# A two-block transformer kernel on one core: the order of the output projections at the end of the first block, and where the second branch's weights are loaded

## The chip, the cores and the metric

The kernel runs on one core of one Trainium2 chip. The metric is the device time of one execution in microseconds. All data is fp32, so each wide matmul of the program stands in the trace as two records.

## The reference

512 tokens of width 1024 go through two blocks. The change lies in the end of the first block's mixing half and the start of its expert half:

```python
merged = gate_a * (y_a @ w_branch_a[l]) + gate_b * (y_b @ w_branch_b[l])
mix = merged @ w_out[l]
x = layer_norm(DN_ALPHA * x + g1 * mix, ln1_g[l], ln1_b[l])
h = layer_norm(x) * (1 + sc2) + sh2
# moe_ffn(h): top 4 of 32 experts for each token
logits = (xt @ w_router).astype(jnp.float32) + b_router
top_v, top_e = lax.top_k(logits, TOP_K)
```

`y_b` is the attention's output (512 wide), `w_branch_b` is 512 x 1024, `w_out` 1024 x 1024, `w_router` 1024 x 32. The assignments are sorted by expert; each expert's rows are then read in blocks of 64. The second block (recurrent and attention mixing, then a product-key expert layer that gathers 128 rows for each token) is not touched.

## The kernel before

Each engine has its own instruction list, written out by hand, and they meet through semaphores. The program is a row of stages (`first_mix`, `first_merge`, `experts`, `second_project`, `second_heads`, `route_peer`); `end_stage` (line 57) clears the stage's semaphores and puts a barrier over all engines between two of them. Transfers that are under way are not waited for by the barrier.

Weights come in units of 512 columns into `ring`, three slots of 2 MB that lie in the same memory as the later expert weights `wt`. In `first_mix` a list of 17 names (line 121) is worked off: unit n goes into slot n % 3, and SP waits until the outputs of unit n - 3 are done (`s_full`). Four outputs of 128 x 512 are made of each unit, 68 in all. The last loop of TensorE takes two of the last eight projections (`gb0`, `gb1`, the second gate) for each of four token tiles, waits for the vector engine's combined attention output of the tile (`s_yb`) and transposes it into `yT[:, 1]`. For each tile SP first reads the three attention groups back from DRAM (line 348); the third read waits for the first tile to be combined, the fourth for the second.

`first_merge` (lines 814 to 1058) then does, with everything loaded anew from its start:

- The branch product: eight groups of 128 rows, four matmuls each (line 892), from `w_branch_b`'s halves in slots 0 and 1. The vector engine multiplies each by the gate and adds it to `mT` (lines 1013, 1014).
- `mixed(t)`, the output projection of token tile t (line 902): two halves of 8 matmuls, into two PSUM banks of its own, from `w_out`'s halves in slots 2 and 0. The second half of `w_out` is issued when the first four branch groups are done.
- `tile(t)` on the vector engine (lines 990 to 999): scales and adds the residual, norm, second norm, and writes `h2`. Each of the two norms sends its variance to ScalarE for a square root (`root(2t)`, `root(2t + 1)`, line 949).
- `logits(t)`: eight transposes of `h2` (line 910), two copies of them on ScalarE (`keep(t)`, line 954), and the router product, 8 narrow matmuls of 32 columns (line 916). `choose(t)` on the vector engine (lines 1003 to 1009) takes the top four and makes a mask.
- `rank(t)`: matmuls with triangular and all-ones matrices that count the assignments before each token (line 927), and in the last tile the total of each expert (line 924). After the last mask the vector engine works out `pos`, the row of each assignment (line 1047).
- GpSimd scatters the rows of `h2` to DRAM, sixteen indirect transfers of 512 KB (line 882). The stage ends when these have landed. SP issues the first expert's twelve weight units of 1 MB (line 870) as soon as the last `mixed` is done, since they lie over `ring` and `mT`.

The orders before: TensorE does mixed 0, mixed 1, logits 0, mixed 2, logits 1, mixed 3, logits 2, rank 0, rank 1, logits 3, rank 2, rank 3. The vector engine does tile 0, tile 1, choose 0, tile 2, choose 1, tile 3, choose 2, choose 3. ScalarE does roots 0, 1, 2, 3, keep 0, roots 4, 5, keep 1, roots 6, 7, keep 2, keep 3.

`experts` begins by reading the first gathered rows and transposing them (line 1144).

Of the kernel before, what the change touches and what calls it, by code (L numbers as in the profile page):

```python
# [13 lines left out]
P = 128  # L14
T = 512
NT = T // P
D = 1024
KD = D // P
W = 512
# [28 lines left out]
TAKEN = []  # L48
# [15 lines left out]
def build(nc, A, K, out, dram):  # L64

    with ExitStack() as ctx:
        def sb(name, shape, dt=F32, c=ctx):
            return c.enter_context(nc.sbuf_tensor(name, shape, dt))

        ident = sb("ident", [P, P])  # L70
        tri = sb("tri", [P, 4, P])
        mod = sb("mod", [P, 6 * D])
        x = sb("x", [P, NT, D])
        ps = ctx.enter_context(nc.psum_tensor("ps", [P, 8, W], F32))
        blocks = sb("blocks", [P, NBLK + 1 + NE], I32)
        pos = sb("pos", [P, NT, TOPK], I32)
        w4 = sb("w4", [P, NT, TOPK])
        with ExitStack() as early:
            wt = sb("wt", [P, NUNIT, 2, D], c=early)
            s_w = [nc.alloc_semaphore(f"e_w{u}") for u in range(NUNIT)]  # L80
            with ExitStack() as first:
                flat = wt[:, :, :, :].rearrange("p u k n -> p (u k n)")
                qkv = flat[:, 0:12 * D].rearrange("p (b a t w) -> p b a t w", b=2, a=3, t=NT)
                ring = flat[:, 12 * D:].rearrange("p (n k w) -> p n k w", n=3, k=KD)
                gB = flat[:, 0:KD * T].rearrange("p (f t) -> p f t", f=KD)
                mT = flat[:, 6 * D:6 * D + KD * T].rearrange("p (f t) -> p f t", f=KD)
                yT = sb("yT", [P, 2, NT, T], c=first)
                hT = sb("hT", [P, KD, T], c=first)
                first_mix(nc, A, K, dram, ident, tri, mod, x, ps, yT, hT, qkv, ring, mT, gB)
                end_stage(nc)  # L90
                first_merge(nc, A, K, dram, ident, tri, mod, x, ps, yT, hT, ring, mT, gB, blocks, pos, w4, wt, s_w)
                end_stage(nc)
            experts(nc, A, K, dram, ident, ps, blocks, wt, s_w)
            end_stage(nc)
        mix = sb("mix", [P, NT, D])
        uv = sb("uv", [P, NRING, 2, D])
        with ExitStack() as second:
            flat = uv[:, :, :, :].rearrange("p n a d -> p (n a d)")
            TA, NA = T + TC, NT + NTC
            ends = [0]  # L100
            for n in (8 * TA, NA * MH * (MD + 1), (NA + NT) * MH * MD, NA * 784):
                ends.append(ends[-1] + n)
            parts = [flat[:, a:b] for a, b in zip(ends, ends[1:])]
            S = dict(ct=parts[0], va=parts[1].rearrange("p (t h c) -> p t h c", t=NA, h=MH), ko=parts[2],
                     zr=parts[3].rearrange("p (t c) -> p t c", t=NA), bg=sb("bg", [P, 16], c=second), flat=flat)
            kept = (NT + NTC) * MH * MD
            S["kt"] = S["ko"][:, 0:kept].rearrange("p (t h c) -> p t h c", t=NT + NTC, h=MH)
            S["om"] = S["ko"][:, kept:].rearrange("p (t c) -> p t c", t=NT)
            second_project(nc, A, K, dram, ident, mod, x, ps, S, mix, pos, w4)
            end_stage(nc)  # L110
            s_wout = [nc.alloc_semaphore(f"q_wout{u}") for u in range(2)]
            second_heads(nc, A, K, dram, ident, tri, mod, ps, S, mix, s_wout)
            end_stage(nc)
        route_peer(nc, A, K, dram, ident, tri, mod, x, ps, mix, out, uv, s_wout)


def first_mix(nc, A, K, dram, ident, tri, mod, x, ps, yT, hT, qkv, ring, mT, gB):

    NB = 3
    names = ["u", "v"] + [f"{a}{g}" for g in range(3) for a in "qkV"] + ["ga0", "wa0", "ga1", "wa1", "gb0", "gb1"]  # L120
# [21 lines left out]
    with ExitStack() as ctx:  # L142
# [6 lines left out]
        with ExitStack() as ctx2:  # L149
# [63 lines left out]
            s_landed = [sem(f"landed{i}") for i in range(NB)]  # L213
# [57 lines left out]
            with nc.Block() as block:  # L271
                @block.sync
                def _(sp):
# [63 lines left out]
                    sp.wait_ge(s_rows, 1)  # L337
                    sp.dma_start(dram["modr"], rows).then_inc(s_rout, 16)
                    sp.wait_ge(s_rout, 16)
                    for b in range(2):  # L340
                        sp.wait_ge(s_out[b], outs_before[b])
                    for t in range(NT):
                        if t >= 2:
                            sp.wait_ge(s_yb, t - 1)
                        else:
                            sp.wait_ge(s_PT, 12)
                            sp.wait_ge(s_o, 12)
                        sp.dma_start(oc[:, t % 2], dram["o"][:, t * P:(t + 1) * P, :].rearrange("g p c -> p g c")
                                     ).then_inc(s_oc[t % 2], 16)

                @block.gpsimd
                def _(pool):
# [458 lines left out]
                        dve.tensor_tensor(y, y, oc[:, t % 2, 2, 0:AH * DH], ALU.add).then_inc(s_yb, 1)  # L811


def first_merge(nc, A, K, dram, ident, tri, mod, x, ps, yT, hT, ring, mT, gB, blocks, pos, w4, wt, s_w):

    NB = 3
    PAD = 16
    with ExitStack() as ctx:
        def sb(name, shape, dt=F32):
# [2 lines left out]
        def sem(name):  # L822
            return take(nc, "g_" + name)
# [24 lines left out]
        sw = small[:, 28:32]  # L848
        posf = small[:, 32:48].rearrange("p (t k) -> p t k", t=NT)

        s_landed = [sem(f"landed{i}") for i in range(NB)]
        s_const, s_back, s_full, s_gate, s_branch, s_mix = (sem(n) for n in ("const", "back", "full", "gate", "branch", "mix"))
        s_dve, s_var, s_sd, s_h2, s_turn, s_h2T = (sem(n) for n in ("dve", "var", "sd", "h2", "turn", "h2T"))
        s_lg, s_ex, s_exp, s_mask, s_rank, s_pos, s_rows = (sem(n) for n in ("lg", "ex", "exp", "mask", "rank", "pos", "rows"))
        with nc.Block() as block:
            @block.sync
            def _(sp):
                for n in range(4):
                    if n >= NB:
                        sp.wait_ge(s_full, 4 * (n - NB + 1))  # L860
                    src = A["w_branch_b" if n < 2 else "w_out"].rearrange("(k p) n -> p k n", p=P)[:, :, n % 2 * W:(n % 2 + 1) * W]
                    sp.dma_start(ring[:, n % NB, 0:src.shape[1]], src).then_inc(s_landed[n % NB], 16)
                    if n == 1:
                        sp.dma_start(x[:, :, :], A["x"].rearrange("(t p) d -> p t d", p=P)).then_inc(s_back, 16)
                        sp.dma_start(mod[:, 2 * D:], dram["modr"].rearrange("r w -> (r w)").unsqueeze(0)[:, 0:4 * D].broadcast_to([P, 4 * D])
                                     ).then_inc(s_back, 16)

                sp.wait_ge(s_full, 8 + 2 * NT)
                for u in range(NUNIT):
                    sp.dma_start(wt[:, u].rearrange("p k n -> p (k n)"), A["w_exp"][0, u]).then_inc(s_w[u], 16)  # L870
# [15 lines left out]
            @block.tensor  # L886
            def _(pe):
                for n in range(2):
                    pe.wait_ge(s_landed[n], 16)
                    for j in range(4):  # L890
                        for k in range(NT):
                            last = nc.tensor.matmul(ps[:, 4 * n + j, :], ring[:, n, k, j * P:(j + 1) * P], yT[:, 1, k, :],
                                                    start=(k == 0), stop=(k == NT - 1))
                        last.then_inc(s_full, 1)
                pe.wait_ge(s_branch, 8)
                pe.wait_ge(s_landed[2], 16)
                pe.wait_ge(s_landed[0], 32)

                def mixed(t):
                    for hf in range(2):  # L900
                        for k in range(KD):
                            last = nc.tensor.matmul(ps[:, 2 * t + hf, :], mT[:, k, t * P:(t + 1) * P], ring[:, (2 + hf) % NB, k, :],
                                                    start=(k == 0), stop=(k == KD - 1))
                        last.then_inc(s_full, 1)

# [24 lines left out]

                mixed(0)
                mixed(1)
                logits(0)
                mixed(2)
                logits(1)
                mixed(3)
                logits(2)
                rank(0)
                rank(1)
                logits(3)  # L940
                rank(2)
                rank(3)

# [1 line left out]
            def _(act):  # L945
                def root(n):
                    t = n // 2
                    act.wait_ge(s_var, n + 1)
                    act.activation(sd[:, t:t + 1], sd[:, t:t + 1], ACT.Sqrt).then_inc(s_sd, 1)
# [4 lines left out]
                        act.copy(h2T[:, 4 * b:4 * b + 4, t * P:(t + 1) * P],  # L954
                                 ps[:, 2 * t + b, :].rearrange("p (k q) -> p k q", k=4)).then_inc(s_h2T, 1)

                for t in range(NT):
                    root(2 * t)
                    root(2 * t + 1)
                    if t >= 1:  # L960
                        keep(t - 1)
                keep(NT - 1)
                act.wait_ge(s_ex, 1)
                act.activation(w4[:, :, :], w4[:, :, :], ACT.Exp).then_inc(s_exp, 1)

# [1 line left out]
            def _(dve):  # L967
# [50 lines left out]
                link(dve.tensor_scalar(thr[:, :], iot[:, 0:T // BLK], float(BLK), None, ALU.mult))  # L1018
                tile(0)
                tile(1)  # L1020
                choose(0)
                tile(2)
                choose(1)
                tile(3)
                choose(2)
                choose(3)
                dve.tensor_tensor(w4[:, :, :], v8[:, :, 0:TOPK], v8[:, :, 0:1].broadcast_to([P, NT, TOPK]), ALU.subtract
# [1702 lines left out]
```

## Time and profile before

| | us |
|---|---|
| median of 3 runs | 3992.58 (3989.98 to 3995.61) |
| span of the profiled execution | 3992.7 |
| TensorE busy | 3398.0 (85%) |
| vector engine busy | 1939.7 (49%) |
| ScalarE busy | 681.1 (17%) |
| GpSimd busy | 935.4 (23%) |
| TensorE's mean granted clock | 0.938 |
| first_merge, from barrier to the last scatter | about 650 to 828 |

The profiled execution's own time is its span, 3992.7 us; nothing else is recorded around it. Times in the rows are microseconds from the start of the span. A granted clock of 1.00 is 2.4 GHz and one of 0.50 is 1.2 GHz; a value between them is a stretch that has some of both.

### The profile page before, as it was taken

To read this page: it belongs to the slowest core of one execution; us is meant where nothing else is said; L and a number is where in the kernel's file an instruction comes from. 1 tells how busy PE (TensorE), PEld (TensorE's weight loads), DVE (VectorE), ACT (ScalarE), POOL (GpSimd) and SP (SyncE) were. 2 spreads that over 40 slices of the span, in tenths; PEclk is the share of its full clock that TensorE was granted. 3 is DMA by queue.
4 is the path that set the end of the run, shared out by engine and by line. 5 is a ranking of instruction groups with operands and counts; after the bars stand their busy time and mean duration, and the time that the engine had idled before them with its cause. 6 is when DMAs were issued, how large, how long until landed. Compare 5 with 4: busy or idle time off the path is not lost. (4 is left out here: it accounts for less than half of the span.)

```text
span 3992.7 us, 37518 instructions
## 1 busy us (share of the span) xinstructions
PE 3398.0 (85%) x11902; PEld 1503.3 (38%) x11903; DVE 1939.7 (49%) x3995; ACT 681.1 (17%) x1601; POOL 935.4 (23%) x810
## 2 busy tenths in 40 slices
PE   7988999768899987999877987788878888787877
PEld 3345444422233322333225555543333333333333
DVE  5834323533233332333325236576666766667676
ACT  1011211000000000000002125312222222222222
POOL 2000000021222212012122022014444344444442
PEclk8999999779999999999998998899989899999998
DMA  9834433269998999196976201149999999999997
GB/s 332 283 110 178 163 109 135 99 254 394 376 385 343 375 397 397 52 381 267 399 286 227 80 7 43 43 182 412 417 421 411 417 408 420 421 399 413 410 421 327
DMA packets 194149, 1157.36 MB, mean 290 GB/s; under 512 B 25659, under 2 KB 27995, under 8 KB 74356
## 3 DMA queue, kind: packets, MB, share of 16 engines
q1 hardware_dynamic: 97140, 565.17, 36.5%
q0 software_dynamic: 80576, 564.05, 34.5%
q10 hardware_dynamic: 16320, 26.75, 2.1%
q8 instruction: 57, 0.93, 0.1%
q14 instruction: 56, 0.46, 0.0%
HBM read 1128.96 MB, written 48.68 MB: 295 GB/s over the span
## 5 line engine op out<-in xcount | busy, mean ns | idle before, releaser
L1156 PE MATMUL ps<-wt,e_xT 128*64 128x512 f32 x3200 | 741.4, 608 | 113.3 <-DMA wt<-in_w_exp 112.4
L2573 DVE SCALAR_TENSOR_TENSOR mod<-uv,mix 128x1024 f32<-128x1024 f32 x512 | 627.2, 1225 | 393.3 <-DMA uv<-in_peer_uv,q_picks 388.1
L2277 POOL DMA_INDIRECT uv<-in_peer_uv,q_picks x512 | 571.9, 1117 | 971.8 <-PE ps L2370 721.0
L2370 PE MATMUL ps<-uv,q_dg 128*128 128x512 f32 x1024 | 533.8, 679 | 147.4 <-ACT q_dg L2447 147.4
L2370 PE MATMUL ps<-uv,tri 128*128 128x512 f32 x1024 | 460.2, 603 | 70.0 <-ACT tri L2447 69.8
L1136 POOL COPY wt<-e_land 128x2048 f32<-128x2048 f32 x124 | 248.1, 2031 | 1000.3 <-PE ps L1156 996.5
L1156 PEld LDWEIGHTS ps<-wt,e_xT 128*64 128x64 f32 x3200 | 219.8, 139 | 593.2 <-issue 383.9
L2370 PEld LDWEIGHTS ps<-uv,q_dg 128*128 128x128 f32 x1024 | 218.5, 219 | 453.6 <-issue 453.6
L1156 PE MATMUL ps<-wt,e_aT 128*64 128x512 f32 x1600 | 354.1, 595 | 3.2 <-ACT e_aT L1209 3.2
L2370 PEld LDWEIGHTS ps<-uv,tri 128*128 128x128 f32 x1024 | 193.1, 192 | 333.5 <-issue 333.5
L461 PE MATMUL ps<-hT,wt 128*128 128x512 f32 x640 | 285.1, 602 | 1.5 <-DVE wt L788 1.5
L1275 DVE TENSOR_TENSOR e_ut<-ps,e_bias 128x512 f32<-128x512 f32 x50 | 34.6, 691 | 401.0 <-PE ps L1156 401.0
L1209 ACT COPY e_aT<-ps 128x512 f32<-128x512 f32 x50 | 29.3, 586 | 1092.0 <-PE ps L1144 1069.6
L1156 PEld LDWEIGHTS ps<-wt,e_aT 128*64 128x64 f32 x1600 | 115.1, 138 | 233.3 <-issue 233.3
L2441 ACT ACTIVATE q_ap<-q_ap 128x4 f32<-128x4 f32 x128 | 26.3, 205 | 932.0 <-DVE mod L2573 932.0
L461 PEld LDWEIGHTS ps<-hT,wt 128*128 128x128 f32 x640 | 120.8, 192 | 151.0 <-issue 145.1
L673 DVE SCALAR_TENSOR_TENSOR x<-mod,small,x 128x512 f32<-128x512 f32 x168 | 129.2, 769 | 32.7 <-DMA mod<-in_w_ada_units 20.8
L1292 DVE TENSOR_TENSOR e_yb<-ps,e_bias 128x512 f32<-128x512 f32 x50 | 34.6, 692 | 172.1 <-PE ps L1156 172.1
L461 PE MATMUL ps<-wt,hT 128*128 128x512 f32 x256 | 116.5, 611 | 0.7 <-ACT hT L563 0.7
L1264 DVE LOAD_MASK_SELECT e_bias<-e_raw x50 | 0.7, 14 | 207.7 <-DMA e_raw<-in_b_exp 160.5
L2326 PE MATMUL ps<-q_hT,q_wq 128*128 128x512 f32 x224 | 98.4, 592 | 0.0
L1437 PE MATMUL ps<-p_ring,p_hT 128*128 128x512 f32 (+1 forms) x256 | 97.4, 542 | 0.0
(452 smaller groups left out, 3428.7 us busy)
## 6 DMA issues: line engine op xcount, KB each, us to landing
wt<-in_w_exp SPq DMA_DIRECT2D x260, 1024.0 KB, 19.2
e_land<-in_w_exp SPq DMA_DIRECT2D x124, 1024.0 KB, 24.0
wt<-in_w_in_units SPq DMA_DIRECT2D x15, 2048.0 KB, 11.1
mod<-in_w_mod_units SPq DMA_DIRECT2D x48, 512.0 KB, 5.6
scratch_xs<-const_zeros SPq DMA_DIRECT2D x8, 2080.0 KB, 9.1
mod<-in_w_ada_units SPq DMA_DIRECT2D x32, 512.0 KB, 7.9
p_ring<-in_w_in SPq DMA_DIRECT2D x7, 2048.0 KB, 10.4
e_xg<-scratch_xs ACTq DMA_DIRECT2D x104, 128.0 KB, 7.0
```

Of the source, the lines that this page charges most:

```text
L461: last = nc.tensor.matmul(ps[:, j, :], lhs, rhs, start=(k == 0), stop=(k == kt - 1))
L673: last = dve.scalar_tensor_tensor(at, quarter[:, q, kk, :], cs[:, v, k:k + 1], at, ALU.mult, ALU.add)
L1136: nc.gpsimd.tensor_copy(wt[:, 8 + u], land[:, u]).then_inc(s_cp[u], 1)
L1156: ins = nc.tensor.matmul(ps[64 * h:64 * h + 64, at, :], lhs[:, k % 4, 64 * (k // 4):64 * (k // 4) + 64], wt[:, u, a, h * W:(h + 1) * W], s ...
L1209: nc.scalar.copy(dst, ps[:, at, :].rearrange("p (k q) -> p k q", k=4)).then_inc(kept, 1)
L1275: link(dve.tensor_tensor(ut[:, :], ps[:, U, :], bias[:, 1, :], ALU.add))
L1292: dve.tensor_tensor(yb[:, :], ps[:, Y, :], bias[:, 3, :], ALU.add).then_inc(s_y, 1)
L1437: last = nc.tensor.matmul(ps[:, m % NBANK, 0:rhs.shape[1]], lhs, rhs, start=(k == 0), stop=(k == KD - 1))
L2277: pool.indirect_dma_start(out=uv[:, slot(n), :, :].rearrange("p a d -> p (a d)"), out_offset=None, in_=A["peer_uv"], in_offset=bass.Indire ...
L2326: last = nc.tensor.matmul(ps[:, 6 + c, :], wq[:, h % 2, k, c * NK:(c + 1) * NK], hT[:, k, :], start=(k == 0), stop=(k == KD - 1))
L2370: last = nc.tensor.matmul(acc(t)[:, c, :], dg(n), uv[:, slot(n), 1, c * W:(c + 1) * W], start=fresh, stop=closing)
L2573: dve.scalar_tensor_tensor(junk[:, n % 2, :], uv[:, slot(n), 0, :], 1.0, mix[:, tile_of(k), :], ALU.mult, ALU.mult, accum_out=ap[:, k % 2, ...
```

## The change

The branch weights are loaded at the end of `first_mix`, into the slots that its unit list would use next (2 and 0), with two semaphores of their own that outlive the barrier. `first_merge` begins with the first half of `w_out` into slot 1, `x`, the modulation vectors, and then, when four branch groups are done, the second half into slot 2. TensorE does mixed 0, 1, 2, logits 0, mixed 3, logits 1, logits 2, rank 0, logits 3, rank 1, 2, 3. The vector engine does tile 0, 1, 2, choose 0, tile 3, choose 1, 2, 3. ScalarE does roots 0 to 3, keep 0, roots 4, 5, keep 1, root 6, keep 2, root 7, keep 3.

```diff
@@ first_mix, SP
                     sp.wait_ge(s_rout, 16)
+                    def branch(u):
+
+                        n = len(names) + u
+                        sp.wait_ge(s_full, 4 * (n - NB + 1))
+                        sp.dma_start(ring[:, n % NB, 0:NT], A["w_branch_b"].rearrange("(k p) n -> p k n", p=P)[:, :, u * W:(u + 1) * W]
+                                     ).then_inc(s_wb[u], 16)
+
                     for b in range(2):
                         sp.wait_ge(s_out[b], outs_before[b])
                     for t in range(NT):
...
                         sp.dma_start(oc[:, t % 2], dram["o"][:, t * P:(t + 1) * P, :].rearrange("g p c -> p g c")
                                      ).then_inc(s_oc[t % 2], 16)
+                        if t == 1:
+                            branch(0)
+                    branch(1)
@@ first_merge, SP
-                for n in range(4):
-                    if n >= NB:
-                        sp.wait_ge(s_full, 4 * (n - NB + 1))
-                    src = A["w_branch_b" if n < 2 else "w_out"].rearrange("(k p) n -> p k n", p=P)[:, :, n % 2 * W:(n % 2 + 1) * W]
-                    sp.dma_start(ring[:, n % NB, 0:src.shape[1]], src).then_inc(s_landed[n % NB], 16)
-                    if n == 1:
+                for u in range(2):
+                    if u == 1:
+                        sp.wait_ge(s_full, 4)
+                    src = A["w_out"].rearrange("(k p) n -> p k n", p=P)[:, :, u * W:(u + 1) * W]
+                    sp.dma_start(ring[:, 1 + u], src).then_inc(s_landed[u], 16)
+                    if u == 0:
@@ first_merge, TensorE
-                    pe.wait_ge(s_landed[n], 16)
+                    pe.wait_ge(s_wb[n], 16)
...
                 mixed(0)
                 mixed(1)
+                mixed(2)
                 logits(0)
-                mixed(2)
+                mixed(3)
                 logits(1)
-                mixed(3)
                 logits(2)
                 rank(0)
+                logits(3)
                 rank(1)
-                logits(3)
                 rank(2)
                 rank(3)
@@ first_merge, ScalarE
-                for t in range(NT):
-                    root(2 * t)
-                    root(2 * t + 1)
-                    if t >= 1:
-                        keep(t - 1)
-                keep(NT - 1)
+                for n in range(6):
+                    root(n)
+                    if n == 3:
+                        keep(0)
+                keep(1)
+                root(6)
+                keep(2)
+                root(7)
+                keep(3)
@@ first_merge, the vector engine
                 tile(0)
                 tile(1)
+                tile(2)
                 choose(0)
-                tile(2)
+                tile(3)
                 choose(1)
-                tile(3)
                 choose(2)
                 choose(3)
```

## Rows read from the trace of the kernel before

**Rows 1.** The page, part 4: the chain that ended last, by engine.
```profile
PE 16%; DMA 15%; DVE 3%; issue 1%; ACT 1%; POOL 0%; DVEq 0%; POOLq 0%
```
**Rows 2.** Timeline of SP's issues, 560 to 800 us: start, length, queue, line, transfer, count.
```profile
593.06 19.68 SPq L348 DMA_DIRECT2D scr<-scratch_o  x4
...
650.02 0.93 SPq L862 DMA_DIRECT2D wt<-in_w_branch_b  x2
...
653.54 20.19 SPq L862 DMA_DIRECT2D wt<-in_w_out  x2
773.61 8.38 SPq L870 DMA_DIRECT2D wt<-in_w_exp  x12
```
**Rows 3.** Timeline of TensorE, 560 to 800 us; in brackets idle time before, what ended it.
```profile
589.58 15.67 PE L461 MATMUL ps<-hT,wt 128*128 128x512 f32 x32 [1.53 <-DVE wt L788]
...
647.60 0.60 PE L547 MATMUL ps<-ident,og 128*128 128x128 f32 x4
656.58 30.48 PE L892 MATMUL ps<-yT,wt 128*128 128x512 f32 x64 [8.38 <-DMA wt<-in_w_branch_b]
688.57 27.73 PE L902 MATMUL ps<-wt 128*128 128x512 f32 x64 [1.50 <-DVE wt L1014]
...
725.59 3.62 PE L916 MATMUL ps<-g_wr,hT 128*128 128x32 f32 x16 [8.41 <-ACT hT L954]
729.02 16.36 PE L902 MATMUL ps<-wt 128*128 128x512 f32 x32
...
787.58 1.95 PE L910 MATMUL ps<-ident,yT 128*128 128x128 f32 x8
...
795.57 1.92 PE L924 MATMUL ps<-g_mask,tri 128*128 128x32 f32 x8 [0.46 <-DVE g_mask L1009]
```
**Rows 4.** Timeline of ScalarE around the first router product.
```profile
724.37 0.20 ACT L949 ACTIVATE g_small<-g_small 128x1 f32<-128x1 f32 x1 [4.62 <-DVE g_small L982]
724.48 1.05 ACT L954 COPY hT<-ps 128x512 f32<-128x512 f32 x2
```
**Rows 5.** Windows: length, busy PE, PEld, DVE, ACT, POOL, granted clock, DMA share, GB/s.
```profile
589.00:595.00 6.00, 5.42 (x9) 2.39 (x10) 2.22 (x4) 0.00 (x0) 0.00 (x0) 0.72 0.36 84
725.00:727.00 2.00, 1.41 (x7) 1.42 (x7) 1.96 (x2) 0.53 (x2) 0.00 (x0) 0.50 0.00 0
2577.00:2578.00 1.00, 1.00 (x4) 0.52 (x4) 0.00 (x0) 0.78 (x2) 0.00 (x0) 1.00 0.78 238
```
**Rows 6.** Timeline of the vector engine, 620 to 803 us.
```profile
622.10 0.18 DVE L798 TENSOR_TENSOR small<-small,scr 128x24 f32<-128x24 f32 x1 [9.25 <-ACT small L629]
...
663.07 0.69 DVE L1013 TENSOR_TENSOR wt<-wt,ps 128x512 f32<-128x512 f32 x1 [22.38 <-PE ps L892]
...
773.61 0.69 DVE L990 TENSOR_TENSOR g_tmp<-ps,mod 128x512 f32<-128x512 f32 x1 [5.45 <-PE ps L902]
...
783.40 1.28 DVE L999 SCALAR_TENSOR_TENSOR yT<-yT,g_small,mod 128x1024 f32<-128x1024 f32 x1
...
793.86 0.19 DVE L1003 TENSOR_TENSOR g_lg<-ps,g_br 128x32 f32<-128x32 f32 x1 [5.68 <-PE ps L916]
...
797.52 0.19 DVE L1031 COPY g_cnt<-ps 128x32 f32<-128x32 f32 x1 [1.93 <-PE ps L924]
...
802.18 0.17 DVE L1047 CAST pos<-g_small 128x16 int32<-128x16 f32 x1
```
**Rows 7.** Timeline of TensorE at the start of route_peer.
```profile
2575.07 1.94 PE L2341 MATMUL ps<-ident,mix 128*128 128x128 f32 x16 [1.78 <-PEq L61]
```
**Rows 8.** DMA issues, 672 to 690 us: transfer, count, KB each, us to landing.
```profile
wt<-in_w_out SPq DMA_DIRECT2D x1, 2048.0 KB, 10.4
```
**Rows 9.** Windows, columns as in rows 5: the units and the scatters.
```profile
773.00:804.00 31.00, 16.64 (x78) 15.44 (x76) 19.23 (x51) 4.04 (x8) 1.34 (x1) 0.58 0.96 392
805.00:806.00 1.00, 0.00 (x0) 0.00 (x0) 1.00 (x1) 0.00 (x0) 0.69 (x2) 0.50 0.09 33
827.00:829.00 2.00, 0.00 (x0) 0.00 (x0) 0.00 (x0) 0.00 (x0) 0.00 (x0) 0.50 0.54 217
```

More of the change, by code:

```diff
@@ L88, in build @@
                 hT = sb("hT", [P, KD, T], c=first)
-                first_mix(nc, A, K, dram, ident, tri, mod, x, ps, yT, hT, qkv, ring, mT, gB)
+                s_wb = [nc.alloc_semaphore(f"g_wb{u}") for u in range(2)]
+                first_mix(nc, A, K, dram, ident, tri, mod, x, ps, yT, hT, qkv, ring, mT, gB, s_wb)
                 end_stage(nc)
-                first_merge(nc, A, K, dram, ident, tri, mod, x, ps, yT, hT, ring, mT, gB, blocks, pos, w4, wt, s_w)
+                first_merge(nc, A, K, dram, ident, tri, mod, x, ps, yT, hT, ring, mT, gB, blocks, pos, w4, wt, s_w, s_wb)
                 end_stage(nc)
@@ L114, in build, with first_mix @@
         route_peer(nc, A, K, dram, ident, tri, mod, x, ps, mix, out, uv, s_wout)
-def first_mix(nc, A, K, dram, ident, tri, mod, x, ps, yT, hT, qkv, ring, mT, gB):
+def first_mix(nc, A, K, dram, ident, tri, mod, x, ps, yT, hT, qkv, ring, mT, gB, s_wb):
     NB = 3
@@ L811, in _, with first_merge @@
                         dve.tensor_tensor(y, y, oc[:, t % 2, 2, 0:AH * DH], ALU.add).then_inc(s_yb, 1)
-def first_merge(nc, A, K, dram, ident, tri, mod, x, ps, yT, hT, ring, mT, gB, blocks, pos, w4, wt, s_w):
-    NB = 3
+def first_merge(nc, A, K, dram, ident, tri, mod, x, ps, yT, hT, ring, mT, gB, blocks, pos, w4, wt, s_w, s_wb):
     PAD = 16
@@ L849, in first_merge @@
         posf = small[:, 32:48].rearrange("p (t k) -> p t k", t=NT)
-        s_landed = [sem(f"landed{i}") for i in range(NB)]
+        TAKEN.extend(s_wb)
+        s_landed = [sem(f"landed{i}") for i in range(2)]
         s_const, s_back, s_full, s_gate, s_branch, s_mix = (sem(n) for n in ("const", "back", "full", "gate", "branch", "mix"))
@@ L888, in _ @@
                 for n in range(2):
-                    pe.wait_ge(s_landed[n], 16)
+                    pe.wait_ge(s_wb[n], 16)
                     for j in range(4):
                         for k in range(NT):
-                            last = nc.tensor.matmul(ps[:, 4 * n + j, :], ring[:, n, k, j * P:(j + 1) * P], yT[:, 1, k, :],
+                            last = nc.tensor.matmul(ps[:, 4 * n + j, :], ring[:, (2 + n) % 3, k, j * P:(j + 1) * P], yT[:, 1, k, :],
                                                     start=(k == 0), stop=(k == NT - 1))
@@ L895, in _ @@
                 pe.wait_ge(s_branch, 8)
-                pe.wait_ge(s_landed[2], 16)
-                pe.wait_ge(s_landed[0], 32)
+                pe.wait_ge(s_landed[0], 16)
+                pe.wait_ge(s_landed[1], 16)
                 def mixed(t):
@@ L901, in mixed @@
                         for k in range(KD):
-                            last = nc.tensor.matmul(ps[:, 2 * t + hf, :], mT[:, k, t * P:(t + 1) * P], ring[:, (2 + hf) % NB, k, :],
+                            last = nc.tensor.matmul(ps[:, 2 * t + hf, :], mT[:, k, t * P:(t + 1) * P], ring[:, 1 + hf, k, :],
                                                     start=(k == 0), stop=(k == KD - 1))
```

## The prediction

> **What bounds the kernel now.** I read the chain that ended last first, and it is of little help here: it names the gathers and matmuls of the last third of the program, and its listed shares add up to about a third of the span [rows 1]. The kernel is a row of stages with a barrier between them, so a stage that is shorter by some microseconds moves everything behind it, unless something in it started at a time that does not move. So I turned to the timelines by engine of the stretch from 588 to 830 us: the end of first_mix, first_merge, and the scatter that ends it. They are to be read for three things: what TensorE waits for, what the vector engine waits for, and when the transfers start. On SP's queue the two halves of w_branch_b go out at the barrier, 650.02 us, the last half of w_out some 20 us after 653.54, and the twelve expert units at 773.61 [rows 2]. On TensorE there are two kinds of holes: 8.38 us at the start, until w_branch_b has landed, and 8.41 us in front of the router products, ended by a ScalarE copy [rows 3]. The reader is to see in ScalarE's rows that the copy (line 954) starts right behind a square root (line 949) of the *next* tile's second norm, which is ahead of it in ScalarE's order [rows 4]: transposes ready since 717 wait until 724.5 for an engine that does nothing. The windows show that the holes cost twice: the granted clock is at its lower level (0.50, 1.2 GHz) in the router products, and the next wide products take 16.36 us where two tiles take 27.73 at full clock [rows 3, 5]. So in this stage TensorE's order is the bound up to the last projection, then the vector engine's chain for tile 3 up to the positions, then the DMA engines (twelve units and sixteen scatters) up to about 828 us.
>
> **Part 1, branch weights begun earlier.** The two 1 MB loads leave the start of first_merge and go into the last loop of first_mix: the first behind the second attention read (that read goes out just after 593), the second behind the fourth (612.7) and behind the wait for gb0's outputs. That wait is met when TensorE has done four of its last eight projections, about 619. Behind the first load on SP's queue stand the third and fourth attention reads. Its own wait is for products that were done before the attention reads began, so it adds only its transfer of 1 MB, 2.7 us at 390 GB/s [rows 9]; the third read goes out near 603, and the vector engine idles 9.25 us in each of these turns [rows 2, 6]. Cost: nothing; without that idle time it would be up to 3 us. Both loads have landed by about 626, so TensorE starts at the barrier. The one other stage that starts with TensorE work right behind a barrier shows it going at once, 1.78 us after its last operation [rows 7]. I take 650.2 in place of 656.58: 6.4 us. The 64 records of the branch product took 30.48 us, of which the first group cost 6.49 (656.58 to the vector engine's 663.07) and the other seven 24.0, or 3.43 each; at full clock it is 8 x 3.43 = 27.5 [rows 3, 6]. Is the clock still up at 650? In the stage start of [rows 7] it was (1.00 two microseconds on); but after 1.53 us of idle time, behind narrow products, at 589.58, it went down while wide products ran, and 32 records took 15.67 instead of 13.9, a loss of 1.8 [rows 3, 5]. I take half of that, 0.9, with 0 and 1.8 as the ends. The wait for the vector engine's last two operations stays at 1.5. The output projections then start at 650.2 + 27.5 + 1.5 + 0.9 = 680.1 instead of 688.57: 8.5 us.
>
> Do the w_out halves land by then? Before, the second was issued near 673.3 (the end of the 20.19 us row) and took 10.4, so it landed near 683.7 [rows 2, 8], through DMA engines that had been full since 651. Now 2 MB of the traffic behind the barrier is gone (5.3 us at 390 GB/s), the first half goes out first, and the second at 4 groups x 3.43 after 650.2, about 664, behind a backlog: it lands at 683.7 - 5.3 = 678.4. That is 1.7 us ahead of the need, so it costs nothing, but it is what is late next; the x rows and the modulation vectors come before it and are wanted 7 us later.
>
> The Trainium skill, TensorE: Matmul & The Clock Gate, section What's actually happening (Part 1), says that the activity measure runs freely, so that the same kernel can have more or fewer slow matmuls in different runs. By that each of my half penalties would be all or nothing from one execution to the next; the rows show both outcomes behind gaps of nearly the same length, which agrees with it.
>
> **Part 2, the order of the projections.** Before, the expert units are issued at 773.61, 85.0 us behind the first projection: four tiles of projection, and between them two router products with their 8.4 us holes. Now three projections run without a gap, then one router product, then the fourth. Four tiles at full clock are 2 x 27.73 = 55.5, less the overlap of the pieces: 55.3. The router product of tile 0 no longer waits: tile 0's h2 is ready some 16 us before it is asked for, and ScalarE's order still has copy 0 behind root 3, but that root is past by some 4 us. It costs 0.7 (transposes to the first copy) + 1.1 (copies from 724.48 to the products at 725.59) + 1.8 (half of 3.62, as that ran at 0.50) = 3.7; with all of it at the lower level it is 6.3, as at 787.58 [rows 3, 4, 6]. Behind it the fourth projection may start at the lower clock as at 589.58; again I take 0.9 of 1.8. Together 55.3 + 4.6 = 59.9 (ends 59.0 and 63.4). The expert units are then issued at 680.1 + 59.9 = 740.0 instead of 773.61: 33.6 us.
>
> The vector engine follows: a tile takes 11.1 us from its second half to h2 (773.61 to 783.40 + 1.28) [rows 6]. Its third tile starts when the second half is there (721.5), not when tile 1 is finished (some 719), and ends at 732.6; choose(0), 1.7 us (793.86 to the rank product at 795.57, which waited for it), ends before the second half of the fourth comes at 740.0. The edit that puts tile 2 ahead of choose(0) is thus hidden behind TensorE. Tile 3 ends at 751.1. Meanwhile TensorE does the router products 1 and 2, each 3.7 to 6.3 us, so choose(1) and choose(2) (3.4 us) are done by 754.5. ScalarE's copies of tile 2 fall between root 6 (about 743) and root 7 (748), each of which takes 0.2; were both router products slow, root 7 would stand behind those copies for up to 1 us. Router product 3 takes 6.3, as TensorE has stood still: 757.4. Then, new on this path, two rank products instead of one stand ahead of the count: ten records of 0.24 at the low clock, 2.45, and the count itself 1.95 [rows 3]; the vector engine has the sum at 761.8. From there to the positions it was 4.8 (797.52 to 802.35) [rows 6]: 766.6 instead of 802.35, 35.8 us earlier.
>
> **What sets the end of the stage.** The DMA engines were full from the issue of the units to the end of the scatters, 773.61 to about 828.1 (window 827 to 829 at 0.54), except for about 1.1 us at 805, where the units were in and the first scatter was not yet moving (0.09) [rows 9]. That is 53.4 us of transfer. Now the positions come 26.6 us behind the issue of the units, not 28.7, so the hole closes, and the end is 740.0 + 53.4 = 793.4. By the other path, positions plus 25.75 (802.35 to 828.1), it would be 766.6 + 25.75 = 792.4. The later of the two counts: 793.4, a gain of 34.7 us. The experts' stage starts from the first gathered rows and is then fed by its own weight stream; nothing in it starts at a time that does not move, so it shifts as a whole, and the later stages with it.
>
> The sum: 3992.7 - 34.7 = 3958.0 in the profiled execution, whose span is within 0.2 us of the median of the timed runs, 3992.58; so 3957.9.
>
> **Rivals.** (a) The second half of w_out is late. For it: only 1.7 us of margin, DMA engines full. If it landed no earlier than before, 683.7, the start would be 683.8, 3.7 later: 3961.6. Against it: 2 MB less traffic ahead of it and an issue 9 us earlier. Chance 0.12. (b) The transfers do not bind the end, since the units' loads give way to the scatters: then the positions' path sets it, and with no low clock at all (0.9 + 0.9 back, router product 3 in 3.7) the end is 792.4 - 4.4 = 788.0, gain 40: 3952.6. The scatters have more to move than what is left of the units, so they finish last in any sharing; that speaks against it. Chance 0.08. The Trainium skill, DMA: Bandwidth & Descriptors, section Issuing engines are not separate DMA queues, says that transfers of all issuers run on the same 16 DMA engines and interleave; by that the sum of both streams counts, as in my forecast, and this rival falls. (c) The gain does not reach the end: the 1.2 ms weight stream or the gathers of the last part run by a rate of their own and give 30 us or more back. A loss of 2.5% in the stream's rate would do. For it only that these stages are the long ones [rows 1]; against it that no transfer of theirs is issued at a fixed time. 3985 to 3996, chance 0.04. (d) The other side: the granted clock goes down in the first gap at 650 and stays down through the whole stage, because each narrow product with its gap lets it fall again. Its place is the branch product and the four projections, 27.5 + 55.3 us of wide work that doubles: +82.8, so 3992.7 - 34.7 + 82.8 = 4041. It makes the kernel slower once more than 35 us of that wide work, about two fifths, runs at the lower level besides what I have counted. For it: the clock did fall after a short gap [rows 5]. Against: it came back within some 4 us there, and under 27.73 us of back-to-back projections it never fell. Chance 0.04.
>
> **How the numbers follow.** The likeliest case, chance 0.72, has its own range from the clock terms: no penalty gives 3956.1, both in full with a router product at the low clock (63.4 - 59.9 + 0.9 = 4.4 more) gives 3962.3. With rivals (a) and (b), and some 2 us for how later stages fall with the clock, the range is 3952.0 to 3966.0. What a measurement of this kernel can tell from no change is about 0.2%, 8 us. Faster by more: 0.92 (0.72 + 0.12 + 0.08). Within it: 0.04, rival (c). Slower by more: 0.04, rival (d).
>
> **What would show it.** In the changed trace: line 892's group starts at the barrier and takes about 27.5 us; the first projection starts near 680, ended by the vector engine and not by a DMA; three tiles of projection without a gap; no idle time of 8 us ahead of the router products; SP issues the units near 740; positions near 767; DMA engines full up to about 793 with no hole; the experts' first transposes near 801 instead of 835.9. Wrong would be: idle time on TensorE ended by w_out (rival a), a start of the branch product later than 652, a clock of 0.50 in the fourth projection throughout, or a shift of the first expert product that is not found again at the end of the program (rival c).

## The result and the profile after

| | before | after |
|---|---|---|
| median, us | 3993.95 (3989.98 to 3995.61, 4 runs) | 3958.81 (3954.63 to 3964.46, 4 runs) |
| ratio | | 0.9915 (95% interval 0.9904 to 0.9927) |
| span of the profiled execution | 3992.7 | 3962.7 |
| barrier to the experts' first transposes | 185.9 (650.02 to 835.89) | 149.0 (650.63 to 799.67) |

The median fell by 35.1 us; the forecast was 3957.9. The device time of the execution whose span is 3962.7 was 3964.46, so some 1.8 us lie around a span; the forecast had taken them for nothing. The last row is the one to work with: the stage that was changed became 36.8 us shorter. (Its start moved by 0.6 us, which is within its wander: over the ten kernels profiled here that barrier comes between 645.7 and 650.6 us.)

TensorE's timeline of the changed kernel, which answers to rows 3 (start, length, engine, line, operation, in brackets the idle time before and what ended it):

```profile
648.22 0.60 PE L558 MATMUL ps<-ident,og 128*128 128x128 f32 x4
650.68 27.70 PE L903 MATMUL ps<-yT,wt 128*128 128x512 f32 x64 [1.86 <-PEq L61]
679.89 41.47 PE L913 MATMUL ps<-wt 128*128 128x512 f32 x96 [1.51 <-DVE wt L1028]
721.19 1.04 PE L921 MATMUL ps<-ident,yT 128*128 128x128 f32 x8
722.96 1.97 PE L927 MATMUL ps<-g_wr,hT 128*128 128x32 f32 x16 [0.73 <-ACT hT L965]
724.76 13.98 PE L913 MATMUL ps<-wt 128*128 128x512 f32 x32
...
743.95 3.00 PE L927 MATMUL ps<-g_wr,hT 128*128 128x32 f32 x16 [0.72 <-ACT hT L965]
746.76 0.61 PE L938 MATMUL ps<-g_mask,tri 128*128 128x32 f32 x2
749.90 1.97 PE L921 MATMUL ps<-ident,yT 128*128 128x128 f32 x8 [2.53 <-DVE yT L1013]
752.55 3.62 PE L927 MATMUL ps<-g_wr,hT 128*128 128x32 f32 x16 [0.67 <-ACT hT L965]
```

Against [rows 3] the reader is to see three things. The branch product starts with the barrier and takes 27.70 us, not 30.48. Three tiles of projection are one group of 96 records, and the idle time ahead of the router product is 0.73 us where it was 8.41. And the fourth projection takes 13.98 us where the two projections behind a hole took 16.36 and 15.48. SP's issues, which answer to [rows 2]:

```profile
594.92 0.48 SPq L345 DMA_DIRECT2D wt<-in_w_branch_b  x1
...
620.07 0.37 SPq L345 DMA_DIRECT2D wt<-in_w_branch_b  x1
...
664.68 0.37 SPq L873 DMA_DIRECT2D wt<-in_w_out  x1
738.77 8.21 SPq L881 DMA_DIRECT2D wt<-in_w_exp  x12
```

The windows, with the columns of [rows 5], which answer to [rows 5, 9]; the third number from the end is the granted clock:

```profile
650.00:653.00 3.00, 2.32 (x6) 1.16 (x7) 0.00 (x0) 1.28 (x1) 1.89 (x3) 1.00 0.28 59
724.00:727.00 3.00, 3.00 (x15) 1.80 (x15) 2.59 (x6) 0.20 (x1) 0.00 (x0) 1.00 0.00 0
742.00:746.00 4.00, 3.27 (x24) 3.04 (x23) 3.67 (x5) 1.26 (x3) 0.00 (x0) 0.83 1.03 424
746.00:752.00 6.00, 3.34 (x15) 2.81 (x14) 5.35 (x17) 0.88 (x3) 0.00 (x0) 0.50 0.99 418
766.00:790.00 24.00, 0.00 (x0) 0.00 (x0) 4.17 (x6) 0.00 (x0) 16.59 (x16) 0.50 1.01 406
790.00:792.00 2.00, 0.00 (x0) 0.00 (x0) 0.00 (x0) 0.00 (x0) 0.00 (x0) 0.50 0.54 219
```

The DMA engines are full from the issue of the expert units to about 791, with no hole where before there was one at 805 [rows 9]. On the vector engine the count and the positions come at 760.05 and 764.72; in [rows 6] it was 797.52 and 802.18:

```profile
760.05 0.19 DVE L1045 COPY g_cnt<-ps 128x32 f32<-128x32 f32 x1 [2.10 <-PE ps L935]
...
764.72 0.17 DVE L1061 CAST pos<-g_small 128x16 int32<-128x16 f32 x1
```

### The profile page after: what moved, and what is told of

It reads as the page before. It is cut to its first block and busy times, and to the rows that moved or that the text cites. A ratio compares the mean times of both kernels' runs of the same rounds, so it can differ in the third digit from the quotient of the medians.

```text
span 3962.7 us, 37518 instructions
## 1 busy us (share of the span) xinstructions
PE 3383.5 (85%) x11902; PEld 1495.0 (38%) x11903; DVE 1939.3 (49%) x3995; ACT 681.2 (17%) x1601; POOL 942.1 (24%) x810
## 3 DMA queue, kind: packets, MB, share of 16 engines
q1 hardware_dynamic: 97140, 565.17, 36.8%
q0 software_dynamic: 80576, 564.05, 34.7%
## 5 line engine op out<-in xcount | busy, mean ns | idle before, releaser
L2384 PE MATMUL ps<-uv,q_dg 128*128 128x512 f32 x1024 | 525.5, 670 | 150.5 <-ACT q_dg L2461 150.5
L1223 ACT COPY e_aT<-ps 128x512 f32<-128x512 f32 x50 | 29.3, 585 | 1095.9 <-PE ps L1158 1073.4
```

What stands on the lines that cost most here:

```text
L2384: last = nc.tensor.matmul(acc(t)[:, c, :], dg(n), uv[:, slot(n), 1, c * W:(c + 1) * W], start=fresh, stop=closing)
```

## The experiments

All distances below count from the stage's barrier (SP's or TensorE's first instruction behind it) in that kernel's own trace, since the barrier itself wanders by 5 us from one profiled execution to another. Each kernel has one trace. Ratios are to the kernel before, run on the same chip.

| | first projection | units issued | positions | experts' first transposes | ratio (95%) |
|---|---|---|---|---|---|
| before | 38.6 | 123.6 | 152.2 | 185.9 | 1 |
| after | 29.3 | 88.1 | 114.1 | 149.0 | 0.9915 (0.9904 to 0.9927) |
| e1, weights only | 29.3 | 113.6 | 142.2 | 176.1 | 0.9974 (0.9964 to 0.9984) |
| e2, order only | 38.9 | 99.5 | 125.4 | 160.2 | 0.9943 (0.9924 to 0.9961) |
| e3, ScalarE's order only | 38.7 | 102.9 | 128.7 | 163.1 | 0.9944 (0.9924 to 0.9964) |
| e4, ScalarE's order back | 29.3 | 88.2 | 116.0 | 149.8 | 0.9914 (0.9894 to 0.9934) |
| e5, units held | 29.3 | 96.4 | 114.1 | 156.8 | 0.9933 (0.9916 to 0.9949) |
| e6, six units early | 29.3 | 29.2 and 88.1 | 114.1 | 147.6 | 0.9913 (0.9896 to 0.9929) |
| e7, early and wide products | 29.3 | 29.2 and 88.1 | 112.8 | 146.6 | 0.9909 (0.9892 to 0.9925) |
| e8, all four first | 29.3 | 29.2 and 84.5 | 113.5 | 147.3 | 0.9908 (0.9891 to 0.9924) |

### e1: the weights alone

The changed kernel with the three orders of before put back (the cut shows TensorE's; ScalarE's and the vector engine's went back too):

```diff
                 mixed(0)
                 mixed(1)
-                mixed(2)
                 logits(0)
-                mixed(3)
+                mixed(2)
                 logits(1)
...
```

> Part 1 alone: the branch weights begin in first_mix, but the orders on TensorE, the vector engine and ScalarE are those of before. My theory: the start of the stage is worth the hole of 6.4 us and the low clock of the first groups (2.8 us), whatever the order behind it; branch product at the barrier, 27.7 us long, first projection about 29.2 us behind the barrier; the 8.4 us holes ahead of the router products stay, and so does the distance of 85 us from the first projection to the issue of the expert units. Positions, last scatter and the end of the program 9 us earlier than before: about 3984. Rival: the DMA engines set the end of the stage, and their work only moved, so less than 5 us arrives.

The stage became 9.8 us shorter than before, the median 3980.66 against 3991.97. Nearly all of it, 9.3 us, is at the front, and TensorE's timeline shows that the holes stay:

```profile
648.08 27.70 PE L903 MATMUL ps<-yT,wt 128*128 128x512 f32 x64 [1.86 <-PEq L61]
677.29 27.73 PE L913 MATMUL ps<-wt 128*128 128x512 f32 x64 [1.51 <-DVE wt L1025]
704.87 1.04 PE L921 MATMUL ps<-ident,yT 128*128 128x128 f32 x8
714.31 3.62 PE L927 MATMUL ps<-g_wr,hT 128*128 128x32 f32 x16 [8.41 <-ACT hT L965]
717.75 15.91 PE L913 MATMUL ps<-wt 128*128 128x512 f32 x32
```

Of the 9.3 us at the front, 6.5 are the wait for the transfer (8.38 us of idle time against 1.86), and 2.8 the clock (30.48 against 27.70). The remaining 0.5 lies in the projections behind the holes, which were 0.7 us shorter than in the trace before. The rival, that the work only moved, falls.

### e2: the orders alone

The kernel before with the orders of the change on TensorE, the vector engine and ScalarE, and `w_branch_b` loaded where it was (the three order hunks of the change, nothing else).

> Part 2 alone: orders of the changed kernel, but w_branch_b loaded at the start of first_merge as before. My theory: branch product starts 6.5 us behind the barrier at the low clock, as before; from the first projection to the issue of the expert units 59 us in place of 85; end of the stage and of the program about 26 to 28 us earlier than before: about 3967. The two parts add up to the whole. Rival: w_out's second half or the positions come too late for it and the parts do not add: less than 22 us.

The stage is 25.7 us shorter, median 3970.68. Here the fourth projection did meet the lower clock: 15.68 us where the changed kernel has 13.98, behind the same 0.73 us gap and the same 1.97 us router product. That is why the units go out 60.6 us behind the first projection and not 58.9:

```profile
656.15 30.17 PE L892 MATMUL ps<-yT,wt 128*128 128x512 f32 x64 [9.05 <-DMA wt<-in_w_branch_b]
...
730.89 1.97 PE L916 MATMUL ps<-g_wr,hT 128*128 128x32 f32 x16 [0.73 <-ACT hT L954]
732.70 15.68 PE L902 MATMUL ps<-wt 128*128 128x512 f32 x32
```

The two parts alone give 9.8 + 25.7 = 35.5 us against 36.8 together. The low stretch in e2 accounts for 1.7 us more, its first projection, which came 0.4 us later behind the barrier than before, for 0.4, and the 0.7 us in e1's projections have to be taken off: 36.9. So the parts add up, and the rival (less than 22 us) falls.

### e3: ScalarE's order alone

```diff
                 for t in range(NT):
+                    if t >= 1:
+                        keep(t - 1)
                     root(2 * t)
                     root(2 * t + 1)
-                    if t >= 1:
-                        keep(t - 1)
                 keep(NT - 1)
```

> The kernel before with ScalarE's order alone changed: the copies of tile t - 1 stand ahead of the two roots of tile t, so that no router product waits for the next tile's norms. TensorE and the vector engine keep their orders, no weights are moved. Theory that the holes are made by ScalarE's order: the 8.4 us holes vanish with this alone, three router products lie inside the projections at 3.7 us each at full clock, the units are issued 55.3 + 2 x 3.7 = 63 us behind the first projection, 22 us earlier than before, and the end comes 20 to 23 us earlier: about 3972. Rival theory, that the projections have to be put ahead of the first router product to hide its chain: the holes stay at several microseconds, and less than 10 us is gained.

One loop on ScalarE takes 22.8 us out of the stage, nearly nine tenths of what all three orders do together. (The medians, 3968.99 here and 3970.68 in e2, are too close to tell the two apart; the stage tells them apart by 2.9 us.) Its TensorE timeline:

```profile
689.00 27.73 PE L902 MATMUL ps<-wt 128*128 128x512 f32 x64 [1.50 <-DVE wt L1014]
716.57 1.04 PE L910 MATMUL ps<-ident,yT 128*128 128x128 f32 x8
718.33 1.97 PE L916 MATMUL ps<-g_wr,hT 128*128 128x32 f32 x16 [0.73 <-ACT hT L954]
720.14 15.68 PE L902 MATMUL ps<-wt 128*128 128x512 f32 x32
...
737.41 1.97 PE L916 MATMUL ps<-g_wr,hT 128*128 128x32 f32 x16 [0.73 <-ACT hT L954]
739.22 13.98 PE L902 MATMUL ps<-wt 128*128 128x512 f32 x32
```

The router product that had waited 8.41 us waits 0.73, with TensorE's list untouched. So the holes were ScalarE's order, and putting the projections ahead is only one of two ways to get the copies off the next tile's roots. What the projections' order adds is one router product less ahead of the fourth projection. This loop together with the early weights was not run; by the stages it would give about 9.8 + 22.8 = 32.6 of the 36.8 us, an estimate.

### e4: ScalarE's order put back in the changed kernel

```diff
-                for n in range(6):
-                    root(n)
-                    if n == 3:
-                        keep(0)
-                keep(1)
-                root(6)
-                keep(2)
-                root(7)
-                keep(3)
+                for t in range(NT):
+                    root(2 * t)
+                    root(2 * t + 1)
+                    if t >= 1:
+                        keep(t - 1)
+                keep(NT - 1)
```

> The changed kernel with ScalarE's order of before: it differs in one place only, copy 2 stands behind root 7. My theory: the order of the projections has already taken the first two copies off the roots, and only router product 2 waits, some 4 us for root 7, in a stretch where TensorE would wait for tile 3 anyway; issue of the units unchanged, router product 3 later by 1 to 2 us, the end of the stage unchanged within 1 us since the DMA engines set it: about 3959, the same as the changed kernel. Rival: the positions set the end, and it comes 2 us or more later.

As expected: router product 2 waits 4.80 us, the positions come 1.9 us later, the end of the stage 0.7 us later, and the time (median 3956.56) can't be told from the changed kernel's. So once the projections stand ahead, the new order on ScalarE is worth no more than that 0.7 us. In ScalarE's rows copy 2 stands right behind root 7:

```profile
742.27 0.20 ACT L960 ACTIVATE g_small<-g_small 128x1 f32<-128x1 f32 x1 [4.62 <-DVE g_small L993]
742.38 1.05 ACT L965 COPY hT<-ps 128x512 f32<-128x512 f32 x2
```

### e5: the expert units held back

```diff
                 sp.wait_ge(s_full, 8 + 2 * NT)
+                sp.wait_ge(s_lg, 3)
                 for u in range(NUNIT):
```

> The changed kernel, but SP waits for the third router product (the semaphore s_lg at 3) before it issues the twelve expert units: about 8.5 us later than in the changed kernel, 97 in place of 88 us behind the barrier; the positions stay where they are, 114 us behind it. Theory of the forecast, that the DMA engines' whole work from the issue of the units on sets the end of the stage: the DMA engines have a hole less, but the last scatter lands 8 us later, and the experts' first transposes come 157 us behind the barrier in place of 149: about 3965. Rival (b), that the positions' path sets it since the units give way to the scatters: the end moves by less than 3 us.

The units went out 8.3 us later, the positions stayed at 114.1, and the stage became 7.7 us longer (median 3965.2). The transfers from the issue of the units on set its end, nearly one for one; rival (b) falls. Its SP row, and then its windows of the DMA engines:

```profile
743.83 8.95 SPq L882 DMA_DIRECT2D wt<-in_w_exp  x12
```

```profile
760.00:795.00 35.00, 0.00 (x0) 0.00 (x0) 6.87 (x12) 0.00 (x0) 17.44 (x16) 0.50 1.02 417
795.00:798.00 3.00, 0.00 (x0) 0.00 (x0) 0.00 (x0) 0.00 (x0) 0.00 (x0) 0.50 0.20 81
```

### e6: six units early

```diff
-                sp.wait_ge(s_full, 8 + 2 * NT)
-                for u in range(NUNIT):
+                sp.wait_ge(s_branch, 8)
+                for u in (0, 1, 2, 5, 6, 7):
+                    sp.dma_start(wt[:, u].rearrange("p k n -> p (k n)"), A["w_exp"][0, u]).then_inc(s_w[u], 16)
+                sp.wait_ge(s_full, 8 + 2 * NT)
+                for u in (3, 4, 8, 9, 10, 11):
                     sp.dma_start(wt[:, u].rearrange("p k n -> p (k n)"), A["w_exp"][0, u]).then_inc(s_w[u], 16)
```

> The changed kernel, but six of the twelve expert units (0, 1, 2, 5, 6, 7, whose memory is free once the branch product is merged) are issued at s_branch 8, some 29 us behind the barrier, where the DMA engines stand idle; the other six as before. Then all units have landed some 15 us behind the fourth projection, 10 us before the positions. Theory: the scatters have the DMA engines to themselves, and the positions' path (22 us of issues on GpSimd from the positions on, and the last landing) sets the end, which stood only 1 to 2 us behind: the end of the stage comes 1 to 2.5 us earlier than in the changed kernel, 147 us behind the barrier, and the program's time can't be told from it (about 3957). Rival: the end was set by the transfers alone, and with half of them gone it comes 5 us or more earlier.

With 6 MB moved into the idle stretch, the DMA engines have an empty stretch ahead of the scatters, and yet the stage is only 1.4 us shorter: the positions' path stands right behind. The rival (5 us or more) falls. Its median, 3956.58, is not told apart from the changed kernel's. In its windows the share of the DMA engines, the number before the last, is 0.00 ahead of the scatters:

```profile
734.00:752.00 18.00, 13.37 (x78) 12.36 (x75) 13.40 (x34) 5.01 (x9) 0.00 (x0) 0.66 0.86 351
752.00:763.00 11.00, 4.77 (x23) 4.63 (x22) 8.34 (x25) 0.21 (x1) 2.76 (x1) 0.50 0.00 0
```

### e7: wide products to keep the clock up

```diff
                 logits(1)
+                wide(2)
                 logits(2)
                 rank(0)
+                wide(2)
                 logits(3)
```

`wide(n)` is n matmuls of 512 columns into a free bank; nobody reads them.

> The kernel with six units early, and four added wide matmuls of 512 columns whose result nobody reads: two ahead of router product 2 and two ahead of router product 3, in the time in which TensorE would wait for tile 3. Theory, that the low clock (0.50 from some 7 us behind the fourth projection on) costs the positions' path 2.6 us in router product 3 and about 1 us in the count: with the wide products the clock stays up, router product 3 takes 3.7 in place of 6.3 us, the positions come 3 to 4 us earlier than with six units early, the end of the stage too. Rival, that short gaps of 0.7 us and narrow products bring the clock down in any case: no change, or 1 us lost to the added matmuls.

Router product 3 ran in 1.97 us in place of 3.62, but the positions came 1.3 us earlier, not 3 to 4. TensorE's timeline, and the windows behind it:

```profile
744.24 3.45 PE L947 MATMUL ps<-hT,ident 128*128 128x512 f32 x4
747.48 1.29 PE L924 MATMUL ps<-ident,yT 128*128 128x128 f32 x8
749.49 1.97 PE L930 MATMUL ps<-g_wr,hT 128*128 128x32 f32 x16 [0.73 <-ACT hT L974]
751.30 2.24 PE L941 MATMUL ps<-g_mask,tri 128*128 128x32 f32 x10
753.35 1.90 PE L938 MATMUL ps<-g_mask,tri 128*128 128x32 f32 x8
```
```profile
744.00:747.00 3.00, 3.00 (x8) 1.41 (x8) 2.87 (x6) 0.00 (x0) 0.00 (x0) 0.60 1.02 431
752.00:756.00 4.00, 4.00 (x21) 4.00 (x20) 1.78 (x9) 0.22 (x1) 0.00 (x0) 0.50 0.03 14
```

The clock was down in the second pair of wide products, 0.60 in that window, so the pair took 3.45 us and not 1.96 and held the transposes back by 1.1 us (100.3 against 99.3 behind the barrier, and tile 3 is no later here); and it was down again for the rank products and the count, 2.24 and 1.90 us against 2.32 and 1.89 in e6. My expectation was too high by both; the direction was right, and the rival had part of it, as the clock did come down behind narrow products.

### e8: all four projections first

TensorE: mixed 0 to 3, logits 0 to 3, rank 0 to 3; the vector engine: tiles 0 to 3, then choose 0 to 3; ScalarE: roots 0 to 5, keep 0, root 6, keep 1, root 7, keep 2, keep 3; units as in e6.

> More of the same: with six units early, all four projections stand ahead of the first router product, all four tiles ahead of choose(0), rank products last, roots and copies of ScalarE to match. Theory: tile 3 is then bound by the vector engine itself and its h2 comes 4.9 us earlier (94.5 us behind the barrier), but three router products follow one another with only narrow work, the clock falls, and they take 12 to 16 us, so router product 3 ends 0 to 6 us earlier and the positions too: end of the stage 0 to 5 us earlier than with six units early. Rival: the router products hidden inside the projections were the point of the order, and with all of them behind it the positions come later than in the changed kernel.

The positions come 0.6 us earlier than in e6. Three router products in a row took 14.0 us (732.12 to 746.12) with the later ones at the low clock, and the fourth starts 98.3 us behind the barrier where it was 99.3. The stage ends less than 0.5 us earlier than in e6, at the low end of the 0 to 5 expected; the rival, positions later than in the changed kernel, falls. The order of the changed kernel was within a microsecond of this one.

No version beats the changed kernel by more than these runs can tell. By the trace e7's stage is the shortest, 2.5 us less than the changed kernel's.

## Why the prediction was right

- **Start of the branch product** (6.4 us forecast): 6.5, shown alone by e1. TensorE started 1.86 us behind its last operation, as [rows 7] had it. The loads in first_mix's last loop cost nothing; TensorE's part of that loop takes 58.0 us in both traces, and the second load had landed 4.9 us after its issue at 620.07, near 625.
- **The clock behind the barrier** (half of 1.8 us lost): nothing lost here, 1.00 in the window, 27.70 us in each trace with the early weights. So the term was 0.9 too careful.
- **w_out's second half** (landing 678.4, 1.7 us ahead of the need): issued at 664.68, 13.9 us to landing (the row below, of the DMA issues of the changed kernel behind 660 us, columns as in rows 8), so 678.6; the projections began at 679.89, released by the vector engine. Rival (a) did not happen, with 1.3 us to spare.

```profile
wt<-in_w_out SPq DMA_DIRECT2D x1, 2048.0 KB, 13.9
```

- **First projection to the issue of the units** (59.9): 58.9. Router product 0 with its transposes took 3.6 us, forecast 3.7 (its three terms, 0.7, 1.1 and 1.8, in fact add up to 3.6); the penalty of 0.9 was 0 in the changed kernel and 1.7 in e2 and e3. The Trainium skill (TensorE: Matmul & The Clock Gate, What's actually happening) says that the activity measure runs freely, and that one kernel can have different numbers of slow matmuls in different runs. The traces agree in so far as the same gap was followed by 13.98 us in some and 15.68 in others, and by both within e3. That one kernel differs from run to run in the same place no run here shows, as each has one trace; and behind the long holes the loss was no fixed amount (15.26 to 16.36 us).
- **Positions** (766.6): 764.9, and by distance from the first projection 85.0 against 86.5 forecast, of which the penalty that did not come is 0.9.
- **End by the transfers** (53.4 us from the issue of the units, forecast end 793.4): 738.8 to about 791.1, 52.3 us. e5 shows the mechanism: hold the units by 8.3 us, and the end moves by 7.7. e6 shows the other path 1.4 us behind it; the forecast had it 1.0 behind. What the forecast did not see is that in the kernel before it was the other path that set the end. From the positions to the experts' first transposes it took 33.7 us there, 33.9 in e1, and 33.5 to 33.7 in e4, e6, e7 and e8; in the changed kernel, e2 and e3 it was 34.4 to 35, and 42.7 in e5, where the transfers come last. So the positions came 38.1 us earlier, and 1.2 of that was lost when the transfers became the later path.
- **Stage** (34.7 us): 36.8. The two clock terms are 1.8 of the difference. The median came within 1 us of the forecast, closer than the stage did; that is luck, since four runs of the changed kernel spread over 10 us.
- **The way to the end.** The shift of the stage is not found whole in the profiled spans (30.0), but it is in the medians (35.1). The other parts of the program wander: over the ten traces the experts' part takes 1253.6 to 1259.2 us, the two stages behind it 476.9 to 486.8, the last one 1417.0 to 1421.4, in no order that goes with the change. The changed kernel's profiled execution was the slowest of its four, with 3.1 us more than before in the experts and 3.6 more in the last stage. Rival (c), by which 30 us or more are given back, is not borne out. Nor is rival (d), by which the kernel becomes slower.

The diagnosis in the first part was right but stopped short: it named ScalarE's order as the reason of the holes and then counted the projections' order as the cure, without asking what the former alone would do. e3 shows that ScalarE's order alone gives 22.8 of the 25.7 us, with TensorE's list untouched; e4 shows that the orders of TensorE and the vector engine, with ScalarE's as before, give all but 0.7 us. Either is enough to free the copies, so their gains do not add.

## What to carry to other kernels

Where an engine that is nearly idle (17% busy) ends the waits of the one that is the bound, look at its order: a copy queued behind a small operation of the next tile made TensorE wait 8.4 us three times, and moving two lines gave nearly as much (22.8 us) as re-planning three engines (25.7). When two paths meet at a barrier, count both before shortening one: here the transfers and the positions came within 1.5 us of each other, so e6, e7 and e8 each won little. And compare stages by their distance from their own barrier; in the spans of this 4 ms program the parts that were not changed varied by 4 to 10 us each.

## What the runs showed of the hardware

The same sequence (eight transposes, 0.73 us of idle time, sixteen narrow products of 1.97 us, then wide products) was followed by a projection of 13.98 us in the changed kernel (granted clock 1.00), e4, e5, e6 and e7, and by one of 15.68 in e2; e3 has one of each. In e7 the clock was down within a pair of back-to-back wide products that had followed narrow work (0.60 in that window, 3.45 us in place of 1.96), up again for router product 3 (1.97 us) and down for the rank products and the count behind it (0.50, with TensorE busy throughout).
